# Expert layer: the next pair's gate and up products ahead of the down products, and the third pair's weights loaded after the first gather

## What is computed

```python
def hier_moe(a, ...):
    ...
    for e in range(N_EXPERTS):                       # 32 experts, hidden width 256
        hdn = jax.nn.silu(x @ w_gate[e]) * (x @ w_up[e])
        y = y + combine[:, e:e + 1] * (hdn @ w_down[e]).astype(jnp.float32)
```

## Time and profile before

| | us |
|---|---|
| median of 3 runs (lowest to highest) | 605.85 (605.27 to 606.26) |
| the profiled execution, its own time | 604.86 |
| its span | 603.1 |
| PE, DVE, ACT, POOL busy | 529.3, 218.8, 169.5, 138.8 |
| expert stage, from the first gate product to the end | 326.8 to 603.1 |

### The profile page before, as it was taken

One profiled execution on the slowest core, in us unless ns is written; L12 is line 12 of the kernel. 1 busy time (PEld: TensorE's weight loads), 2 busy tenths in 40 slices (PEclk: granted clock), 3 DMA queues, 4 the chain that ended last, 5 costly groups with the idle time before them and its releaser, 6 DMA issues.

```text
span 603.1 us, 9578 instructions
## 1 busy us (share of the span) xinstructions
PE 529.3 (88%) x3304; PEld 390.6 (65%) x3305; DVE 218.8 (36%) x602; ACT 169.5 (28%) x421; POOL 138.8 (23%) x230
## 2 busy tenths in 40 slices
PE   5899999999989999999967888699988799897864
PEld 4888988987657677788866645366645456554431
DVE  4753243242667755427772111111121111211011
ACT  6833333332534333125432201111121011211010
POOL 0132232222513300004536022212202222222212
PEclk9999999999999999999998999899999979999898
DMA  8741000012323111199978499999999999999994
GB/s 323 293 113 37 3 33 1 2 68 77 106 71 96 44 36 36 35 344 420 409 254 316 152 326 386 364 381 383 365 385 384 418 393 378 356 363 369 357 342 120
DMA packets 33447, 140.83 MB, mean 233 GB/s; under 512 B 10488, under 2 KB 11147, under 8 KB 21350
## 3 DMA queue, kind: packets, MB, share of 16 engines
q1 hardware_dynamic: 25776, 124.33, 53.5%
q0 software_dynamic: 5856, 12.60, 8.7%
q10 hardware_dynamic: 1766, 3.25, 1.4%
HBM read 131.15 MB, written 16.46 MB: 245 GB/s over the span
## 4 chain that ended last, share of the span: by engine, by line
DMA 42%; PE 11%; issue 1%; DVE 1%; ACT 1%; POOL 0%; ACTq 0%; SPq 0%; DVEq 0%; POOLq 0%
DMA expert_w<-in_w_gate 19%; DMA expert_w<-in_w_up 19%; DMA token_gates<-gate_rows 4%; PE ps L871 4%; PE ps L508 1%; PE ps L509 1%; PE ps L513 1%; PE ps L887 1%; PE ps L767 1%; PE ps L756 1%; POOL out L1695 0%; PE ps L899 0%; DVE hid L1526 0%; ACT s_act L1158 0%; DVE h_sb L1371 0%
## 5 line engine op out<-in xcount | busy, mean ns | idle before, releaser
L871 PE MATMUL ps<-expert_w,xT 128*64 128x256 f32 x1152 | 130.4, 383 | 18.2 <-DMA expert_w<-in_w_gate 6.0
L871 PEld LDWEIGHTS ps<-expert_w,xT 128*64 128x64 f32 x1152 | 96.9, 138 | 55.3 <-issue 19.4
L887 PE MATMUL ps<-expert_w,hT 128*64 128x512 f32 x272 | 66.0, 628 | 20.6 <-DVE hT L1533 14.8
L1689 POOL DMA_INDIRECT out<-y_sb,idx_now x17 | 27.2, 1597 | 161.6 <-issue 121.5
L1526 DVE SCALAR_TENSOR_TENSOR hid<-s_act,gate,ps 128x256 f32<-128x256 f32 x18 | 12.0, 666 | 141.1 <-ACT s_act L1158 141.1
L887 PEld LDWEIGHTS ps<-expert_w,hT 128*64 128x64 f32 x272 | 22.5, 143 | 53.4 <-issue 48.4
L1158 ACT ACTIVATE s_act<-ps,gate 128x256 f32<-128x256 f32 x18 | 8.5, 474 | 132.6 <-PE ps L871 132.6
L508 PE MATMUL ps<-w_in_hi,aT_hi 128*128 128x384 f32 (+2 forms) x120 | 43.7, 369 | 0.0
L509 PE MATMUL ps<-w_in_lo,aT_hi 128*128 128x384 f32 (+2 forms) x120 | 40.8, 345 | 0.0
L1538 DVE COPY y_sb<-ps 128x512 f32<-128x512 f32 x18 | 12.5, 692 | 77.3 <-PE ps L887 72.9
L1163 ACT ACTIVATE y_sb<-ps 128x512 f32<-128x512 f32 x18 | 10.8, 597 | 81.8 <-PE ps L887 77.9
(11 more groups left out here) (227 smaller groups left out, 932.4 us busy)
## 6 DMA issues: line engine op xcount, KB each, us to landing
expert_w<-in_w_gate SPq DMA_DIRECT2D x32, 1024.0 KB, 9.5
expert_w<-in_w_up SPq DMA_DIRECT2D x32, 1024.0 KB, 9.4
expert_w<-in_w_down SPq DMA_DIRECT2D x30, 1024.0 KB, 9.8
w_in_raw<-in_w_in SPq DMA_DIRECT2D x8, 608.0 KB, 9.9
w_out_raw<-in_w_out SPq DMA_DIRECT2D x8, 512.0 KB, 3.9
token_rows<-h_sb ACTq DMA_DIRECT2D x6, 512.0 KB, 8.4
out<-h_sb SPq DMA_DIRECT2D x6, 512.0 KB, 10.5
x_sb<-in_x_prompt SPq DMA_DIRECT2D x4, 512.0 KB, 11.6
```

Of the source, the lines that this page charges most:

```text
L871: mm = pe.matmul(ps[r, GU_BANK[q.o], g * FH:(g + 1) * FH], xT[:, q.o, k, r], w_gu(b, lane, k, g), start=(k == 0), stop=(k == KD - 1))
L887: mm = pe.matmul(ps[r, 4 + half, :], hT[:, q.o, k, r], w_dn(b, lane, k, half), start=(k == 0), stop=(k == 1))
L1689: pool.indirect_dma_start(out=out, out_offset=bass.IndirectOffsetOnAxis(ap=idx, axis=0), in_=y_sb[:, buf, :], in_offset=None, compute_op=A ...
```

## The change

1. **PE order.** Pair 0's gate and up products move ahead of the loop over the pairs. Then pair j does: transposes of the rows of pair j + 1, transposes of pair j's hidden values, gate and up products of pair j + 1, down products of pair j. The first part of a further pass of pair j + 1 comes at the end of pair j. In pair 0 the transposes of the further pass stand between gate and up.
2. **SP order.** All 6 parts of pair 2 wait for the first gather. Then gate and up of pair j are issued, and after them down of pair j - 1. For j = 3 there is no down part. The last pair's down halves stand behind pair 14's down parts.
3. **Gathers.** Four gathers are started before the last `gate_row` (pairs 0, 1, further pass, 2) in place of two; in the loop POOL gathers pair j + 3 in place of j + 2, and waits for the transposes of pair j.
4. **Routing.** The further pass's slots get a PSUM bank of their own, their indices are made right after those of the main pass, and the 8 small products stand later.
5. ACT and DVE follow: silu and hidden product of pair j + 1 ahead of the copies of pair j's result.

The diff, cut to its core:

```diff
@@ SP: loads
-            load_pair(sp, 2, 2, range(4))
             sp.wait_ge(main.gathered[0], 16)
-            load_pair(sp, 2, 2, range(4, 6))
+            load_pair(sp, 2, 2)
...
 def load_last_down(j, b):
-                    sp.wait_ge(part_in[1 + n], 16 * (j + 1))
+                    sp.wait_ge(part_in[3 + 2 * n], 16 * (j + 1 - n))
...
+            def refill(j, b, first=False):
...
+                used(main.g_mm, j - 2, over.g_mm, passes)
+                sp.wait_ge(part_in[3], 16 * j)
+                load_part(0, j, b)
+                sp.wait_ge(part_in[4], 16 * (j - 1))
+                load_part(1, j, b)
+                used(main.gu_mm, j - 2, over.gu_mm, passes)
+                sp.wait_ge(part_in[5], 16 * (j - 1))
+                load_part(2, j, b)
+                sp.wait_ge(part_in[0], 16 * (j + 1))
+                load_part(3, j, b)
+                if not first:
+                    used(main.y_mm, j - 3, over.y_mm, earlier)
+                    sp.wait_ge(part_in[1], 16 * (j + 1))
+                    load_part(4, j - 1, (b + 2) % 3)
+                    sp.wait_ge(part_in[2], 16 * (j + 1))
+                    load_part(5, j - 1, (b + 2) % 3)
@@ PE: pairs
             def pair(j, i, b, last):
-                gate_up(main, b, j)
+                nb = (b + 1) % 3
+                if not last:
+                    gather_transposes(main, g_rows[:, nb, :], main.gathered[nb], i + 1 if b < 2 else i + 2)
+                hidden_transposes(main, j)
+                if not last:
+                    gate_up(main, nb, j + 1)
...
-                todo = first_pass(j, opening)
-                if not last:
-                    nb = (b + 1) % 3
-                    gather_transposes(main, g_rows[:, nb, :], main.gathered[nb], i + 1 if b < 2 else i + 2)
-                hidden_transposes(main, j)
                 ... down products ...
-                rest_passes(todo, closing, again)
+                rest_passes(overflow(j), closing, again)
+                if not last:
+                    first_pass(overflow(j + 1), opening)
@@ POOL
             gather(g_rows[:, 1, :], table, idx_all[:, 1:2], main.gathered[1])
+            pool.wait_ge(idx_done, 4)
+            gather(more_rows[:, :], table, idx_more[:, 0:1], first_more_in)
+            gather(g_rows[:, 2, :], table, idx_all[:, 2:3], main.gathered[2])
             gate_row(NT - 1)
...
-                    gather_pair(j + 2, (b + 2) % 3, 2 * j + 1)
+                    pool.wait_ge(main.x_tr, j + 1)
+                    gather_pair(j + 3, b, 2 * j + 1)
```

More of the change, by code:

```diff
@@ L315, in rest @@
                             eng.reg_add(before, before, 1)
-            return first, rest
+            return overflow, first, rest
         def y_free(eng, q, n):
@@ L454, in _, with load_part @@
             sp.reg_mov(more, 0)
+            def load_part(n, j, b):
+                what, lane = n // 2, n % 2
+                k = 2 if what == 2 else KD
+                src = a[("w_gate", "w_up", "w_down")[what]][0, bass.ds(PAIRS * lane + j, 1)].rearrange("e (p k) f -> p (e k f)", k=k)
+                sp.dma_start(weights[b][:, lane, what, :], src).then_inc(part_in[n], 16)
             def load_last_down(j, b):
@@ L469, in refill @@
                 passes = sp.snap(more)
-                def used(kind):
-                    sp.wait_ge(kind(main), j - 2)
-                    sp.wait_ge(kind(over), passes)
-                    sp.sem_inc(refill_go, 1)
-                used(lambda q: q.g_mm)
-                load_pair(sp, j, b, range(2))
-                used(lambda q: q.gu_mm)
-                load_pair(sp, j, b, range(2, 4))
-                used(lambda q: q.y_mm)
-                if isinstance(j, int):
-                    load_last_down(j, b)
-                else:
-                    load_pair(sp, j, b, range(4, 6))
-            with sp.Fori(1, PAIRS // 3) as i:
+                used(main.g_mm, j - 2, over.g_mm, passes)
[14 more added lines that the diff above has]
+                    load_part(5, j - 1, (b + 2) % 3)
+            for b in range(3):
+                refill(3 + b, b, b == 0)
+            with sp.Fori(2, PAIRS // 3) as i:
                 for b in range(3):
@@ L489, in _ @@
             refill(PAIRS - 1, 0)
+            used(main.y_mm, PAIRS - 3, over.y_mm, sp.snap(more))
+            load_last_down(PAIRS - 1, 0)
         @block.tensor
@@ L1562, in pair @@
                 hT_copy(main, j)
+                if not last:
+                    hidden(main, j + 1, nb)
                 y_copy(main, j, b, last)
-                rest_passes(todo, closing, again)
+                rest_passes(overflow(j), closing, again)
+                if not last:
+                    first_pass(overflow(j + 1), opening)
             gates(0, 0)
             x_copy(main, 0)
+            hidden(main, 0, 0)
+            first_pass(overflow(0), opening)
             run_pairs(dve, pair)
@@ L1713, in more_gather, with first_more_place, first_more_gate @@
                 pool.tensor_copy(gate[:, 3:4, :], more_gate[:, bass.ds(j, 1), :]).then_inc(over.gate_done, 1)
+            def first_more_place(j):
+                pool.tensor_copy(idx_now[:, 6:7], idx_more[:, bass.ds(j, 1)]).then_inc(more_set, 1)
+            def first_more_gate(j):
+                pool.tensor_copy(gate[:, 3:4, :], more_all[:, bass.ds(j, 1), :]).then_inc(over.gate_done, 1)
             def first_more_gather(j):
@@ L1724, in first_more_gather @@
                     gather(more_rows[:, :], table, idx_now[:, 6:7], over.gathered[0])
-                    pool.tensor_copy(gate[:, 3:4, :], more_all[:, bass.ds(j, 1), :]).then_inc(over.gate_done, 1)
+                    first_more_gate(j)
             def more_add(j, n):
```

204 lines of the change are left out of this document (118 added, 86 removed).

## The result

The changed kernel took **627.81 us** (median of 4 runs, 626.80 to 629.50) against 606.06 (605.27 to 610.83) of the kernel before in the same comparison: a ratio of **1.035, 95% interval 1.031 to 1.040**. Forecast were 609.5 and a range of 603.5 to 613.5. The direction was right, the size was not: +21.8 us in place of +3.7. The profiled execution of the changed kernel took 627.14, its span is 625.5 (603.1 before).

A forecast was written before the change was run, and what follows sets the result against it. The weight stream was taken as the bound, with PE below it. Front terms of -1.25, +1.4, +2.4 and -2.0 gave +0.6 us; with the end's exposed add the span grew 3.7, giving 609.5 from the median, range 603.5 to 613.5.

The forecast's parts named there:

- The bound: Whole kernel: the weight stream sets the time; PE needs about 13.4 us per pair against the stream's 19.3.
- part 3: SP's order: stream runs dry before pair 4's gate, +2.4 us; later down parts give -2.0; PE's 13.2 per pair stays below 19.3.
- the sum: All terms to the end of the span: 606.8 against 603.1 us, 3.7 slower; 609.5 from the median.
- (B): Rival: PE's clock drops after waits before the first gate product and pair 14's down products, 1.7 + 2.2 us, 613.4; chance 0.17.
- Part 1: Holding back pair 2's weights: first gather starts 316.9, lands 321.4; the stream's hole is moved, not removed; -1.25 us.
- the 1.25 for pair 3's gather: Front of the stream: pair 3's gather, a pair earlier, leaves the full stream, the hold-back's one gain, -1.25 us.
- Part 2: Release of buffer 0: first gate product at 327.2, pair 3's gate issued at 341.9, +1.4 us.
- upper bound of +3: Upper bound for the release of buffer 0, if PE's clock falls in the wait before the first product.
- gain of 2.0 for the down parts: SP's order: down parts behind pair 4's gate and up avoid an earlier near-dry stream, -2.0 us, bounds 0 to -3.8.
- Part 4: The end: stream ends at 592.9, pair 14's add is exposed at 6.3 us, last step 7.05, span ends at 606.8.
- (D): Rival: gathers a pair ahead make the stream denser, up to 7 us shorter over ten pairs, 602.5; chance 0.20.
- (C): Rival: the end costs less, exposed add 4 us instead of 6.3, or the front gains 2: 606.4; chance 0.18.

The follow-up runs named there:

- no_third: Changed kernel with the code of third and later passes, never run with this input, left out of PE's program: 613.02 us, ratio 1.009.
- hold_only: Kernel before with one edit, all six parts of pair 2's weights wait for the first gather: 607.35 us, ratio 1.001.
- clock_no_third: Changed kernel, all passes still in despite the label, with fill products ahead of the first gate products and pair 0's further pass: 623.12 us, ratio 1.026.
- before_double: Kernel before with a second, never entered copy of a third pass's code in PE's program: 685.07 us, ratio 1.128.

## Why the prediction was wrong, point by point

**The bound.** "PE needs less than the stream" rested on means: 13.4 against 19.3 us per pair. The step that failed is this one, and its repetition in part 3, that PE's "13.2 per pair ... stay below 19.3". The 13.2 was 13.8 for a plain pair, which is near. What failed is that a plain pair is not all. A further pass, the stops in branches (27.5 us in sum, PE idle for 16.7 of them) and slow products (the groups of 32 and 64 on the trace take 16 us more than at full clock, 1.7 before) come on top: the gate and up products of pairs 2 to 6 start at 377.51 and on to 450.61, 18.3 us apart, where the kernel before has 13.4 for pairs 4 to 6 (402.26 to 429.10). That is close to the stream's own pace, and a PE that is late stays late. The trace of before already showed PE behind the weights: between 491 and 545 no wait of it is longer than the 1.2 us for the hidden values. PE's stops cost 15 of the 21.8 us, as no_third shows. Without the third pass's code the change costs 6 us, still more than the 3.7 of the sum but inside the stated range; so the sum was 2 us short for a kernel without most of the stops, and it had no term for the stops themselves.

**A row read wrongly.** Rival (B) rests on the 3.97 us of idle time ahead of 387.11, whose row names a weight part as what ended it, and does not ask further. The trace of before has PE's branch at the loop's entry from 381.14 to 386.63 there, and pair 3's gate parts had been issued at 340.48. It was the one stop for code that PE already stood idle in, and the slow 8.81 behind it was its second price.

**Part 1, hold-back: right.** First gather started at 317.56 (316.9 forecast), pair 2's first part issued at 322.00 on its landing (321.4), the hole of 331 filled. hold_only shows the hold-back itself to be worth nothing; the 1.25 for pair 3's gather is not in that run and was not tested.

**Part 2, release of buffer 0: right to the first product, then too small.** The first product came at 327.51 (327.2). Pair 3's gate was issued at 345.52 and not at 341.9. Of these 3.6 us, 0.3 are the first product's, 1.7 the slow first 32 products (5.36 for 3.67) and 1.7 the slow further pass, whose first half took 5.2 us in place of 3.5. The longer wait for the further rows' copies, 2.49 where before it was 1.41, is the 1.0 that the forecast had for their transposes. The upper bound of +3 was meant for the clock in one place; it struck in two, and +5.0 was measured.

**Part 3, SP's order: the dry stretch right, the sum not.** The stream ran dry ahead of pair 4's gate (358 to 362, forecast near 353) for 2.7 us against 2.4. The gain of 2.0 for the down parts could not be seen on its own; at pair 5's gate the kernel is 8.2 behind, of which 5.0 came with pair 3. The other 3.2, where +0.4 was forecast, hold the unforecast dry stretch of 378 to 384, which follows on PE's stop of 5.18 us at 369.07. (A small slip: one whole and one short add are 2.4 in the price of the volume and 2.7 here.)

**Part 4, the end: the terms were right, the chain was not.** The exposed add took 6.84 (6.3), the last step 7.08 (7.05). But the sum let pair 14's down products begin as their weights landed. In no_third their last part landed at 588.4 and they began at 592.46, behind pair 15's gate and up products, because PE was late. Of the 9.6 us by which the end is longer, some 5.5 were in the sum; the rest is put down to PE's lateness. The last part landed near 607.5 where 592.9 was forecast, past the 597 that the prediction had named as a sign of being wrong; the mean of pairs 5 to 15, 19.5 us, stayed within 0.3 of 19.3.

**The rivals.** (B), the clock, had its mechanism right, with a price of 3.9 for two places. There were eight groups of slow products, four of them behind a long branch. In the first pair, taking it away gave 4.7 us (clock_no_third) with the long stops there, and 0 to 2 without them. (D), the denser stream, came true in part and is what hid some of the damage: from pair 9 to pair 15 the changed kernel took 109.1 us, before 113.7. (C) did not happen; the row of 6.3 was the better guide than the fit of the Trainium skill's "DMA: Bandwidth & Descriptors", section "Anatomy of one DMA — SWDGE (gpsimd) path", whose estimate of 3.2 is half of the 6.84 measured. A rival "more or worse placed jumps on PE" was missing, though the row for it, the loop's branch of 5.49 us at 381.14 in the kernel before, was in its trace.

**What stays open.** How the last 6 us above before in no_third divide among the end, the clock and the loop's entry: each is worth 0 to 2, all together 5. How much code a jump may pass over before it stops PE was not measured, nor how long a turn of the loop may be before it is fetched again; only that leaving out a third pass's code takes all stops but the loop's entry away, and that a second copy of it makes the branches six times as long in sum (19 long ones in place of 6, in all turns in place of the first). Why the stream between pairs 9 and 15 is denser was not tested.

## What to carry to other kernels

When control flow stays in a kernel, the code that is skipped can have a price on the engine that skips it. Put a jump where the engine still has issued work to do or would wait anyway, avoid two jumps back to back, and keep a never-taken general case as short as it can be, above all in a loop whose turn might no longer be kept. "Issue" as a releaser is a question and not an answer: here it was a branch in most cases, but also a wait for weights or for copies. The sequencer's branches and semaphores in the same stretch tell which. Slack is to be read where the buffers are at their emptiest, as starts with no wait in front of them, not as a mean per turn.

## What the runs showed of the hardware that was not expected

- A branch on PE's sequencer took up to 5.9 us in these kernels and 7.88 in before_double, while the branches on ACT, DVE and POOL took under 0.1.
- In the kernel before and the changed one the long branches (and the 16 KB packets of code) end with the loop's first turn, fetched with 8 packets; in before_double, with 10 packets a turn, they come in every turn.
- Code that never runs moved the time from 607 to 685 us when it was added on PE in one place, and from 628 to 613 when it was left out in another.
- 64 products of 64x128 by 256 columns took 7.13 us at the full granted clock and 8.5 to 10.0 behind a stop of PE. The branch of 5.2 us at 369.07 and the slow group behind it (9.50) cost PE 7.6 us together.
